# Inverse square roots of all norms: half the negative logarithm through the exponential, and one refining step

## The reference

```python
def rms_norm(x, g):
    xf = x.astype(jnp.float32)
    y = xf * lax.rsqrt(jnp.mean(xf * xf, axis=-1, keepdims=True) + NORM_EPS)
    return (y * g.astype(jnp.float32)).astype(x.dtype)
...
    o = rms_norm(o, sub_g) * (1.0 - lambda_init)          # heads of the differential attention
...
    h = rms_norm(x, norm_g)                                # second block, whole rows
    q = (_rms_norm(c_q, q_norm_g) @ w_uq)                  # latents, 768 columns; c_kv has 256
    q = _rms_norm(q, qk_q_g)                               # each head of 96; k the same
    y = jax.nn.silu(_layer_norm(y, ln_g, ln_b))            # behind the convolution
    v = _layer_norm(jax.nn.gelu(v), ln_g, ln_b)            # gated unit
    y = jnp.concatenate([_rms_norm(y_conv, g_conv), _rms_norm(y_mla, g_mla), _rms_norm(y_sg, g_sg)], axis=-1)
    return x + y @ w_out
```

## Time and profile before

| | us |
|---|---|
| median of 3 executions | 1737.08 (1736.78 to 1738.13) |
| the profiled execution | 1732.94 |
| its span, first to last instruction | 1731.2 |
| mean granted TensorE clock in it | 0.938 of full speed |
| the four MLPs, each | some 175, in which TensorE is busy throughout |
| second block, two layers | 1353 to 1728 |

### The profile page before, as it was taken

One profiled execution on the slowest core, in us unless ns is written; L12 is line 12 of the kernel. 1 busy time (PEld: TensorE's weight loads), 2 busy tenths in 40 slices (PEclk: granted clock), 3 DMA queues, 4 the chain that ended last, 5 costly groups with the idle time before them and its releaser, 6 DMA issues. The chain is left out here.

```text
span 1731.2 us, 21281 instructions
## 1 busy us (share of the span) xinstructions
PE 1535.6 (89%) x8735; PEld 1324.5 (77%) x8735; DVE 962.1 (56%) x1177; ACT 802.5 (46%) x1170; POOL 165.1 (10%) x165
## 2 busy tenths in 40 slices
PE   7877999999889999877999997779999787698778
PEld 5655899987679998666999875559998676587666
DVE  4554545465565445654544555445555487668754
ACT  5346543344344434433433454444444454565463
POOL 2000000000000000000000000000000295009700
PEclk9987999999899999998999998879999898899878
DMA  8212355543225554321555551224555422253220
GB/s 300 102 49 98 146 195 194 193 156 137 98 98 195 195 194 163 113 89 50 195 195 183 179 184 52 95 97 168 180 186 194 142 86 91 81 183 122 92 98 25
DMA packets 100612, 241.91 MB, mean 140 GB/s; under 512 B 2642, under 2 KB 11644, under 8 KB 100540
## 3 DMA queue, kind: packets, MB, share of 16 engines
q1 hardware_dynamic: 98848, 237.25, 38.3%
q0 software_dynamic: 1344, 3.52, 1.0%
q10 hardware_dynamic: 348, 0.13, 0.0%
HBM read 239.84 MB, written 1.05 MB: 139 GB/s over the span
## 5 line engine op out<-in xcount | busy, mean ns | idle before, releaser
L1218 DVE TENSOR_TENSOR wlo<-raw,whi 128x2048 fp32r<-128x2048 f32 (+3 forms) x240 | 509.8, 2160 | 239.2 <-ACT whi L498 238.9
L498 ACT ACTIVATE whi<-raw 128x2048 fp32r<-128x2048 f32 (+3 forms) x240 | 418.8, 1790 | 171.2 <-PE pair L859 169.8
L857 PE MATMUL pair<-whi,xhi 128*128 128x512 f32 (+2 forms) x752 | 315.1, 419 | 50.4 <-DVE wlo L1218 35.4
L858 PE MATMUL pair<-wlo,xhi 128*128 128x512 f32 (+2 forms) x752 | 302.5, 402 | 0.0
L859 PE MATMUL pair<-whi,xlo 128*128 128x512 f32 (+2 forms) x752 | 300.8, 400 | 0.0
L857 PE MATMUL pair<-xhi,whi 128*128 128x256 f32 x1024 | 290.9, 284 | 6.9 <-DVE xlo L1247 6.9
L859 PE MATMUL pair<-xhi,wlo 128*128 128x256 f32 x1024 | 289.7, 283 | 0.0
L858 PE MATMUL pair<-xlo,whi 128*128 128x256 f32 x1024 | 289.7, 283 | 0.0
L857 PEld LDWEIGHTS pair<-whi,xhi 128*128 128x128 f32 x752 | 153.4, 204 | 88.9 <-DVE wlo L1218 40.1
L857 PEld LDWEIGHTS pair<-xhi,whi 128*128 128x128 f32 x1024 | 196.3, 192 | 10.4 <-issue 6.9
L857 PE MATMUL pair<-whi,ahi 128*128 128x512 f32 x512 | 199.8, 390 | 0.0
(11 more groups left out here) (233 smaller groups left out, 1658.2 us busy)
## 6 DMA issues: line engine op xcount, KB each, us to landing
raw<-in_mlp_w_up SPq DMA_DIRECT2D x32, 2048.0 KB, 7.9
raw<-in_mlp_w_down SPq DMA_DIRECT2D x32, 2048.0 KB, 7.5
raw<-in_diff_w_in SPq DMA_DIRECT2D x11, 2048.0 KB, 7.8
raw<-in_w_in SPq DMA_DIRECT2D x10, 2048.0 KB, 7.8
raw<-in_moba_w_in SPq DMA_DIRECT2D x6, 2048.0 KB, 7.7
raw<-in_diff_w_out SPq DMA_DIRECT2D x4, 2048.0 KB, 7.7
raw<-in_w_uq SPq DMA_DIRECT2D x4, 1152.0 KB, 5.5
raw<-in_moba_w_out SPq DMA_DIRECT2D x2, 2048.0 KB, 7.7
```

Source lines behind the costliest of these rows:

```text
L498: act.activation(whi[:, s, cols], raw[:, s, cols], ACT.Copy).then_inc(*t["hi_split"].one())
L857: pe.matmul(dst, x_hi, w_hi, start=first, stop=False)
L858: pe.matmul(dst, x_hi, w_lo, start=False, stop=False)
L1218: dve.tensor_tensor(wlo[:, s, cols], raw[:, s, cols], whi[:, s, cols].bitcast(FP32), ALU.subtract)\
```

## The change

Every inverse root is formed in another way. ScalarE takes the logarithm of the mean of squares plus EPS (`Ln`, the scale 1/w and a bias tile `eps` in the activation itself), waits for its own result, and writes `guess` = exp(-0.5 x). VectorE makes the variance as before, waits for `guess`, and refines once in `refined`: guess (1.5 - 0.5 var guess guess), four dependent instructions in place of one reciprocal. ScalarE no longer waits for the variance: with rows and heads it waits for its own sums, with `prepare` and `layer_norm` for VectorE's sums or statistics. GpSimd fills `eps` at the start, and TensorE, which waited for seven constants of GpSimd, waits for eight. All 29 places where a root is taken are changed.

```diff
+            def inverse_roots(dst, log, parts):
+
+                for (at, n, w), src in parts:
+                    m = act.activation(log[:, at:at + n], src, ACT.Ln, scale=1.0 / w, bias=eps[:, 0:1])
+                m.then_inc(*t["log_taken"].one())
+                act.wait_ge(*t["log_taken"].now())
+                some = slice(parts[0][0][0], at + n)
+                return act.activation(dst[:, some], log[:, some], ACT.Exp, scale=-0.5)
+
+            def roots(widths, at=0):
+
+                act.wait_ge(*t["squares_summed"].now())
+                parts = []
+                for n, w in widths:
+                    parts.append(((at, n, w), ss[:, at:at + n]))
+                    at += n
+                inverse_roots(guess, lnv, parts).then_inc(*t["guess_ready"].one())
+
+            def root_of_variance():
+
                 act.wait_ge(*t["var_ready"].after())
-                act.activation(std[:, at:at + n], var[:, at:at + n], ACT.Sqrt).then_inc(*t["std_ready"].one())
+                inverse_roots(guess, lnv, [((6, TT, 1), bn2[:, :, 1])]).then_inc(*t["guess_ready"].one())
...
                     m.then_inc(*t["heads_squared"].one())
-                    roots16(4, 4 * q)
+                    act.wait_ge(*t["heads_squared"].now())
+                    roots16(4, P, 4 * q)
...
-            def roots16(n, at=0):
-                act.wait_ge(*t["sum16_ready"].after())
-                act.activation(std16[:, at:at + n], ss16[:, at:at + n], ACT.Sqrt).then_inc(*t["std16_ready"].one())
+            def roots16(n, w, at=0):
+
+                inverse_roots(guess16, lnv16, [((at, n, w), ss16[:, at:at + n])]).then_inc(*t["guess16_ready"].one())
...
+            def refined(dst, x, y, factor):
+
+                chain(dve.tensor_tensor(factor, y, y, ALU.mult))
+                chain(dve.tensor_tensor(factor, factor, x, ALU.mult))
+                chain(dve.tensor_scalar(factor, factor, -0.5, 1.5, ALU.mult, ALU.add))
+                return dve.tensor_tensor(dst, factor, y, ALU.mult)
+
...
                 if root:
-                    m.then_inc(*t["var_ready"].one())
-                    dve.wait_ge(*t["std_ready"].after())
-                    dve.reciprocal(rstd[:, some], std[:, some]).then_inc(*t["rstd_ready"].one())
+                    chain(m)
+                    dve.wait_ge(*t["guess_ready"].after())
+                    refined(rstd[:, some], var[:, some], guess[:, some], fix[:, some]).then_inc(*t["rstd_ready"].one())
```

More of the change, by code:

```diff
@@ L179, in build @@
         var = sb("var", [P, 12])
-        std = sb("std", [P, 12])
+        lnv = sb("lnv", [P, 12])
+        guess = sb("guess", [P, 12])
+        fix = sb("fix", [P, 12])
         rstd = sb("rstd", [P, 12])
         ss16 = sb("ss16", [P, 32])
-        std16 = sb("std16", [P, 32])
+        lnv16 = sb("lnv16", [P, 32])
+        guess16 = sb("guess16", [P, 32])
+        fix16 = sb("fix16", [P, 32])
+        var16 = sb("var16", [P, 32])
         rstd16 = sb("rstd16", [P, 32])
@@ L187, in build @@
         snk = sb("snk", [P, 8, 2, 2])
+        eps = sb("eps", [P, 1])
         sums = sb("sums", [P, 8, 2, 2])
@@ L549, in norm @@
                 if root:
-                    roots(TT)
+                    roots([(TT, D)])
             def results(p, dst, w, scale):
@@ L719, in second @@
                         sum_squares([qkv[:, tt, c:c + w] for c, w in ((CQ0, QL), (CKV0, KVL)) for tt in range(TT)], 2)
-                        roots(4, 2)
+                        roots([(2, QL), (2, KVL)], 2)
                         act.wait_ge(*t["rstd_ready"].after())
@@ L728, in second @@
                         t.emptied[4].n += 1
-                        roots(TT, 6)
+                        root_of_variance()
                         act.wait_ge(*t["ln_ready"].after())
@@ L740, in second @@
                             .then_inc(*t["heads_squared"].one())
-                        roots16(16, 16 * n)
+                        act.wait_ge(*t["sum16_ready"].after())
+                        roots16(16, QK2, 16 * n)
                     elif what == "gelu":
@@ L767, in second @@
                                         [ypad[:, ct, CONV_K - 1:] for ct in range(2)])
-                            roots(4, 8)
+                            roots([(TT, CW), (TT, SGW)], 8)
                         else:
                             sum_squares([branch(1)[:, tt, :] for tt in range(TT)], 2, [yacc[:, :, :].rearrange("p a b -> p (a b)")])
-                            roots(TT, 2)
+                            roots([(TT, MLAW)], 2)
                         t["rstd_ready"].n += 1
@@ L1462, in roots16 @@
                 some = slice(at, at + n)
-                dve.tensor_scalar(ss16[:, some], ss16[:, some], 1.0 / w, EPS, ALU.mult, ALU.add).then_inc(*t["sum16_ready"].one())
-                dve.wait_ge(*t["std16_ready"].after())
-                return dve.reciprocal(rstd16[:, some], std16[:, some])
+                chain(dve.tensor_scalar(var16[:, some], ss16[:, some], 1.0 / w, EPS, ALU.mult, ALU.add))
+                dve.wait_ge(*t["guess16_ready"].after())
+                return refined(rstd16[:, some], var16[:, some], guess16[:, some], fix16[:, some])
             def add_out(n):
@@ L1518, in layer_norm @@
                     m = dve.bn_aggr(bn2[:, tt, :], bn6[:, tt, :])
[L1519 to L1522, removed]
+                m.then_inc(*t["var_ready"].one())
+                dve.wait_ge(*t["var_ready"].now())
+                chain(dve.tensor_scalar(var[:, 6:6 + TT], bn2[:, :, 1], EPS, None, ALU.add))
+                dve.wait_ge(*t["guess_ready"].after())
+                some = slice(6, 6 + TT)
+                chain(refined(rstd[:, some], var[:, some], guess[:, some], fix[:, some]))
                 for tt in range(TT):
@@ L1550, in prepare @@
                 dve.wait_ge(*t["heads_squared"].after())
-                chain(dve.tensor_reduce(ss16[:, 16 * n:16 * n + 16].rearrange("p (t h) -> p t h", t=TT), squares, AXIS.X, ALU.add))
+                dve.tensor_reduce(ss16[:, 16 * n:16 * n + 16].rearrange("p (t h) -> p t h", t=TT), squares, AXIS.X, ALU.add)\
+                    .then_inc(*t["sum16_ready"].one())
+                dve.wait_ge(*t["sum16_ready"].now())
                 chain(roots16(16, QK2, 16 * n))
@@ L1806, in _ @@
             pool.memset(band[:, :], 0.0).then_inc(*t["pool_step"].one())
+            pool.memset(eps[:, :], EPS).then_inc(*t["consts_made"].one())
             pool.wait_ge(*t["pool_step"].now())
```

5 lines of the change are left out of this document (2 added, 3 removed).

## The result

The changed kernel takes 1766.68 us in the median (1765.61 to 1768.58, 4 runs), the kernel before 1736.93 in the same comparison (1735.8 to 1738.13, 4 runs): ratio 1.0172, 95% interval 1.0159 to 1.0185. The forecast was 1766, in a range of 1755 to 1780. Its profiled execution took 1768.58 us, span 1766.8; that of before 1732.94, span 1731.2. The profiled pair differs by 35.6 us where the medians differ by 29.8: before's profiled execution is 4.0 us under its median, and that of the changed kernel, the longest of its four, 1.9 over.

A forecast was written before the change was run, and what follows sets the result against it. TensorE, busy 1535.6 of 1731.2 us, bounds it, so only root latency it waits for counts: 0.2 + 8.8 + 1.7 + 3.3 + 6.2 + 6.2 = 26.4, plus clock 3, is 29 us on 1737.1: 1766 us, range 1755 to 1780 (0.80).

The forecast's parts named there:

- Diff outputs, 8.8 and 1.7: Layers 0 and 3: second and third outputs cost 2.2 us each, together 8.8; layer 0's fourth 1.7; the rest free.
- the first norm: First norm of the first block: 0.1 to 0.2 us, since ScalarE then waits for a transfer; 0.2 in the sum.
- Covered norms of layers 1 to 3: Row norms: longer roots covered by TensorE's other work, cost 0; layers 1 and 3 by 0.2 us only, layer 2 more.
- Final norm, 3.3: Final norm of the first block: no cover, 0.64 us from variance to scaling becomes 3.95, so 3.3 us more.
- Second block, first layer, 6.2: Convolution's norm 0.7, second preparation 2.0, root of two branches 2.3, third branch 1.2; places ahead of GpSimd's convolution free.
- Second layer, 6.2: Second block: GpSimd starts 2.4 us later, then 0.6, 2.0 and 1.2; the root of two branches free; together 6.2.
- Clock, 3: TensorE's clock: more waiting brings 29 us more at half clock, costing 0 to 14.5 us; 3 taken.
- (a): Rival: much is covered, second-block places overlap; only 18.4 us sure, below that 1741 to 1755 us; chance 0.07.
- (b): Rival: the change is fully hidden behind other work, 1737 us; chance 0.02.
- (c): Rival: clock costs over 14 us, or norm covers break and free second-pass places aren't free: above 1780 us; chance 0.07.
- (d): Rival: one table holds logarithm and exponential, no load between them or ahead of the softmax: 1737 us, no change; chance 0.02.
- The price of a change of set: Added loads on the path: 1.28 us each taken from the trace; the page's 2.66 would add 1.38 each, some 15.

The follow-up runs named there:

- e7: The kernel before, with the new inverse root only at the seven places of the second block that the prediction gave nothing: 1736.56 us, ratio 1.0005.
- e3: The kernel before, with the new inverse root at the eight diff outputs alone (layers 0 and 3): 1751.73 us, ratio 1.0088.
- e10: The kernel before, with the one-set logarithm and exponential at the diff outputs alone, refining step in three instructions: 1742.68 us, ratio 1.0032.
- e11: The kernel before, with only four small VectorE instructions (0.8 us) added behind the second preparation's root in the second block's first layer: 1742.72 us, ratio 1.0043.
- e5: The one-set kernel e1, with each load of the set put ahead of the wait of the first logarithm needing it: 1745.63 us, ratio 1.0058.
- e6: The kernel e5 without VectorE's refining step, the exponential's value only copied: 1738.43 us, ratio 1.0012.
- e2: The kernel before, with the new inverse root at the final norm of the first block alone: 1739.55 us, ratio 1.0026.
- e1: The changed kernel, with logarithm and exponential from one table set, kept for the softmax too, 20 loads instead of 71: 1747.85 us, ratio 1.0069.

## Why the prediction held, point by point

- **Diff outputs, 8.8 and 1.7.** The chain took 4.02 for 3.98. The waits at the second outputs rose by 2.26 and 2.25, at the third by 2.77 and 2.97 (there TensorE had waited 2.33, not the 3.05 that the prediction read as the same), together 10.3 for the forecast 8.8. The 1.7 at the fourth output of layer 0 didn't come: TensorE got to its transposes only at 183.84, when the evictions (from 182.60) were done, since the 24 matmuls ahead of them took 7.2 us instead of 5.6, the first seven standing 0.43 us apart instead of 0.23. The fourth outputs' waiting for the softmax rose by 0.63 and 0.55 and other waits fell. In sum 10.4 us more waiting in the two layers, forecast 10.7 with the first norm.
- **Covered norms of layers 1 to 3.** No new wait, though the cover was judged at 0.2 us.
- **Final norm, 3.3.** The wait went from 6.96 to 10.30, and alone the change there costs 4.1.
- **Second block, first layer, 6.2.** The start to GpSimd's turn was given 0 and took 0.39; e7 shows that the places there are covered. The second preparation was to lengthen one wait by 2.0, to 8.5. Its chain took 2.81 (sums ready at 1494.61, scaling at 1497.42), forecast 2.8, and from the end of the wait ahead of the projection (1489.50) to the end of this one (1504.02) it is 14.5 us, before 12.5: 2.0 more, as forecast. But the wait itself rose only from 6.49 to 7.02, since TensorE was 1.5 us longer at its own work ahead of it. The wait at 1489.50, 1.04 before, is 2.26. The roots of two branches, forecast 2.3, show as a wait of 2.00 for VectorE's scaling (the row at 1528.00), where TensorE had none before, and from the second softmax tile of the stretch to the last (1518.97 to 1532.90, before 1495.41 to 1506.90) it is 2.4 us longer. From 1528.00 to 1545 TensorE's granted clock is 0.50, where it was 1.00 before at the same transposes and softmax tiles, and its next three waits are 2.0 shorter together. So a chain's price can stand in busy time, and the layer's 3.9 us of waiting hide part of it. The third branch's wait is 1.18, forecast 1.2.
- **Second layer, 6.2.** A new wait of 1.67 behind the norm, GpSimd's turn 2.3 later within the layer (forecast 2.4), the third branch 1.29 (forecast 1.2). In waiting 6.2.
- **Instructions.** ScalarE got 33 activations more besides the loads, not 29: the roots of the latents and of the two branches take two logarithms each. Nothing hangs on it.
- **Clock, 3.** This term was mis-sized. Waiting grew by 23.0 in the profiled pair, 3.4 less than forecast; 29.8 by the medians leaves some 7 us for the clock. That the two errors cancel, and the total comes within 1 us, is luck. The step that failed is the rule of three behind the term, that more waiting lowers the clock in proportion and that busy engines absorb most of it. In e3 layer 2 and in e10 the second block's first layer lose 2.25 and 6.4 us with no changed instruction; e11 loses 6.9 in one layer with no more new waiting ahead of it than 0.84. e5 and e6 lose it while waiting less.
- **Rivals.** (a) and (b), cover, are out by e2 and the traces; (c) is out by the time, though its mechanism, the clock, was worth half of its threshold. (d), the shared set, is out for this program, with 29 loads between logarithm and exponential. e1 and e5 make it true by force: 20 loads, and TensorE's waiting is within 1.0 us of before's in every stretch of the first block. Even so its 1737 isn't reached: 1745.6. The waits agree with (d), the clock is what (d) left out.
- **The rule on sets.** That one set holds both functions (the Trainium skill, "ScalarE: Activation LUTs", Table sets: the hidden batching unit) is right by e1. The one load that the Trainium skill gives there for a logarithm and an exponential behind it came only when the set was named: until then this program had two at each root.
- **The price of a change of set.** The Trainium skill ("ScalarE: Activation LUTs", What ACT_TABLE_LOAD costs) gives 2.66 us. The trace after shows 1.28 for each of the roots' 58 loads, 0.02 or less ahead of it, and the next activation 0.02 behind it or less at the 50 where nothing else is waited for. The trace's price carried the sum.

## What to carry to other kernels

Look in the built program at which table loads stand between dependent activations, and force the common set, ahead of the wait, before replacing a function: here 51 of the 71 loads were avoidable, and taking them away took 29.8 us of loss down to 9.7. That is still no gain: in this program no form of the new inverse root was shown to be faster than before. Price a chain from the trace's own rows and add it only where TensorE's wait names it; here the chains that were read came out within about 0.1 us, while the waits for them rose by 0.5 to 3.0 us for the 2.0 to 2.2 forecast at the diff outputs and the preparation. Do not read a difference of several microseconds (6.5 for a delay of 0.8 here) as the price of a chain in a kernel whose attention passes sit between the two clock levels: cut the trace into stretches and separate waiting from busy time first, and test with a delay that computes nothing.

## What the runs showed of the hardware

- A delay of 0.8 us moved one stretch of attention from a granted clock of 1.00 to 0.58 and made its layer 6.9 us longer; one of 2.4 us made it 9.5 longer and gave 5.9 back in the next layer. What decides the level stays open: the waits between the delayed one and the stretch are alike.
- Each ACT_TABLE_LOAD took 1.28 us, the 45 of before and the 71 after. It cost nothing where it stood ahead of a wait that lasted longer (at 1429.18 in before's trace; the root behind it waited 2.57 us more for its variance); behind the wait all of it was on the path: TensorE waits 8.51 us at the second preparation in e1 and 7.23 in e5.
- VectorE's refining instructions, 0.16 each in the first block, took up to 0.62 us in the second block while GpSimd's convolution ran (0.49 in the row at 1438.26 above, 0.62 at 1452.08 in the same trace). No run takes GpSimd away, so that the two share something is argued, not shown.
